# A 2x2 block of gate/up weight chunks in seven products: a macaron SwiGLU block with a mixer, 256 tokens

## The reference

```python
D_MODEL, SEQ, FFN_DIM, N_DIFF_HEADS, DEPTH = 2048, 256, 5632, 8, 1

def rms_norm(x, g):
    return x * lax.rsqrt(jnp.mean(x * x, axis=-1, keepdims=True) + 1e-6) * g

def swiglu(x, w_gate, w_up, w_down):
    return (jax.nn.silu(x @ w_gate) * (x @ w_up)) @ w_down

x = x + 0.5 * swiglu(rms_norm(x, ffn1_norm), ffn1_w_gate, ffn1_w_up, ffn1_w_down)
proj = rms_norm(x, mix_norm) @ w_in                  # 6 parts: b, c, xv, q, k, v
y_conv = short_conv_mixer(b_gate, c_gate, xv, conv_w)
y_attn = rms_norm(diff_attention(q, k, v, lam), subln_w) * (1 - lambda_init)
x = x + jnp.concatenate([y_conv, y_attn], -1) @ w_out
x = x + 0.5 * swiglu(rms_norm(x, ffn2_norm), ffn2_w_gate, ffn2_w_up, ffn2_w_down)
return rms_norm(x, final_norm)                       # (1, 256, 2048), float32
```

## Time and profile before

| | |
|---|---|
| median of 3 runs | 1829.52 us (1829.44 to 1829.53) |
| span of the profiled execution | 1827.1 us |
| around the span, to the median | 2.4 us |
| TensorE busy | 1816.5 us, 99%, 8105 matmuls |
| VectorE busy | 1015.8 us, 56% |
| ScalarE busy | 829.3 us, 45% |
| GpSimd busy | 31.3 us, 2% |
| DMA | 368 MB, mean 201 GB/s |

### The profile page before, as it was taken

One profiled execution on the slowest core, in us unless ns is written; L12 is line 12 of the kernel. 1 busy time (PEld: TensorE's weight loads), 2 busy tenths in 40 slices (PEclk: granted clock), 3 DMA queues, 4 the chain that ended last, 5 costly groups with the idle time before them and its releaser, 6 DMA issues.

```text
span 1827.1 us, 22464 instructions
## 1 busy us (share of the span) xinstructions
PE 1816.5 (99%) x8105; PEld 1500.3 (82%) x8105; DVE 1015.8 (56%) x1237; ACT 829.3 (45%) x986; POOL 31.3 (2%) x36
## 2 busy tenths in 40 slices
PE   9999999999999999999999999999999999999998
PEld 7888888888888888888888888888888888888886
DVE  6555555555545555557657766555555555554554
ACT  6444444444444444545455455444444444443443
POOL 0000000000000000000000000000000000000000
PEclk9999999999999999999999999999999999999999
DMA  7666666666666656765665566666666666655554
GB/s 258 206 207 202 203 205 206 206 203 202 206 205 207 204 195 202 224 190 179 191 207 173 192 208 209 202 205 204 206 206 199 208 203 204 209 199 195 193 195 139
DMA packets 207563, 368.03 MB, mean 201 GB/s; under 512 B 19600, under 2 KB 37648, under 8 KB 207376
## 3 DMA queue, kind: packets, MB, share of 16 engines
q1 hardware_dynamic: 206784, 365.51, 63.2%
q0 software_dynamic: 144, 1.05, 0.2%
q10 hardware_dynamic: 576, 0.69, 0.1%
HBM read 347.25 MB, written 2.10 MB: 191 GB/s over the span
## 4 chain that ended last, share of the span: by engine, by line
PE 99%; DVE 0%; ACT 0%; DMA 0%; issue 0%; DVEq 0%; ACTq 0%
PE bank L382 33%; PE bank L384 33%; PE bank L383 33%; PE bank L508 0%; PE bank L525 0%; DMA x<-in_x_dram 0%; PE bank L420 0%; PE bank L439 0%; PE bank L516 0%; PE bank L533 0%; ACT x L629 0%; DVE w_lo L814 0%; ACT w_hi L596 0%; DVE xT_lo L834 0%; DVE xT_hi L1028 0%
## 5 line engine op out<-in xcount | busy, mean ns | idle before, releaser
L814 DVE TENSOR_TENSOR w_lo<-raw,w_hi 128x1024 fp32r<-128x1024 f32 x655 | 806.4, 1232 | 774.2 <-ACT w_hi L596 773.7
L596 ACT ACTIVATE w_hi<-raw 128x1024 fp32r<-128x1024 f32 x655 | 693.7, 1060 | 910.1 <-PE bank L384 905.3
L382 PE MATMUL bank<-w_hi,xT_hi 128*128 128x512 f32 x1788 | 699.3, 391 | 1.0 <-DVE w_lo L814 1.0
L384 PE MATMUL bank<-w_hi,xT_lo 128*128 128x512 f32 x1788 | 696.1, 389 | 0.0
L383 PE MATMUL bank<-w_lo,xT_hi 128*128 128x512 f32 x1788 | 695.8, 389 | 0.0
L382 PEld LDWEIGHTS bank<-w_hi,xT_hi 128*128 128x128 f32 x1788 | 335.6, 188 | 72.4 <-issue 3.8
L384 PEld LDWEIGHTS bank<-w_hi,xT_lo 128*128 128x128 f32 x1788 | 335.6, 188 | 70.1
L383 PEld LDWEIGHTS bank<-w_lo,xT_hi 128*128 128x128 f32 x1788 | 335.7, 188 | 68.8
L382 PE MATMUL bank<-w_hi,hT_hi 128*128 128x512 f32 x704 | 273.9, 389 | 0.0
L383 PE MATMUL bank<-w_lo,hT_hi 128*128 128x512 f32 x704 | 273.9, 389 | 0.0
L384 PE MATMUL bank<-w_hi,hT_lo 128*128 128x512 f32 x704 | 273.9, 389 | 0.0
(11 more groups left out here) (115 smaller groups left out, 418.2 us busy)
## 6 DMA issues: line engine op xcount, KB each, us to landing
raw<-in_ffn_w_up_dram SPq DMA_DIRECT2D x176, 512.0 KB, 3.7
raw<-in_ffn_w_down_dram SPq DMA_DIRECT2D x176, 512.0 KB, 3.6
raw<-in_ffn_w_gate_dram SPq DMA_DIRECT2D x175, 512.0 KB, 3.5
raw<-in_w_in_dram SPq DMA_DIRECT2D x96, 512.0 KB, 4.2
raw<-in_w_out_dram SPq DMA_DIRECT2D x32, 512.0 KB, 4.1
turn_in<-gate SPq DMA_DIRECT2D x448, 32.0 KB, 2.5
x<-in_x_dram SPq DMA_DIRECT2D x3, 512.0 KB, 8.7
out_dram<-x SPq DMA_DIRECT2D x6, 256.0 KB, 2.8
```

The lines of the kernel that those rows point to most:

```text
L382: pe.matmul(acc, hi[:, kt, ts], w_hi[slot][:, kk], start=(k == 0 and kk == 0), stop=False)
L384: mm = pe.matmul(acc, lo[:, kt, ts], w_hi[slot][:, kk], start=False, stop=(k == chunks - 1 and kk == KC - 1))
L596: act.activation(w_hi[slot][:], raw[slot][:], ACT.Copy).then_inc(hi_ready, 1)
L814: dve.tensor_tensor(w_lo[slot][:], raw[slot][:], w_hi[slot][:].bitcast(F32), ALU.subtract)\
```

## The change

In groups 1 to 8 of each FFN the last two chunks of the width (KA, KB) are taken for gate and up together as a 2x2 block: rows KA, KB and columns gate, up, called b11 (gate, KA), b12 (up, KA), b21 (gate, KB), b22 (up, KB), against the 2x2 block of token tiles by KA, KB. The four block results come from seven products of 6 matmuls (P1 to P7), each on one stationary pair and one combined weight block, and not from eight. Every product has a w_hi and w_lo of its own in the rings of four, so a group has 19 forms: 12 plain ones with 12 matmuls and 7 products with 6.

VectorE builds the combined blocks in place (`outer_sums`, `first_sum`, `second_sum`, `third_sum`) and, once per FFN, the combined token tiles `s_hi`, `s_lo` (`token_sum`, `split_tokens`, in group 0). Some products belong to more than one result. Their sums so far are copied from PSUM by ScalarE (`snapshot`, four copies a group) to tiles `gate_kept` and `up_kept` while the bank goes on accumulating, and are added when the banks are drained (`gate_sum`, `up_sums`); TensorE waits for those copies at three places (`snapped`). The Silu reads the summed tile, and its product with up is one more VectorE step. The four block tiles and the kept tiles lie over the last three groups' part of `hT`, the token sums over `gfin`, whose load moves from the end of the first FFN to the start of the last stage. SP loads a group's blocks during the up phase of the group before, and moves the hidden tile in 4 DMAs behind the first up chunk and 12 behind the second. The loops over groups are unrolled on all engines; groups 0, 9 and 10 keep their form. The turning of a hidden tile moves to the end of its group, for group 0 and the mixed ones. Left out below: ring numbers in unchanged stages, the plain form (as `unit` before) and the token sums' arithmetic.

```diff
+NORM = CD - 2
+KA, KB = CD - 2, CD - 1
+P1, P2, P3, P4, P5, P6, P7 = range(1, 8)
+G0, G1, G2, AT_P1, G3, AT_P5, AT_P2, G4, AT_P6, AT_P4, G5, AT_P7, AT_P3, U0, U1, U2, U3, U4, U5 = range(19)
+AT = {P1: AT_P1, P2: AT_P2, P3: AT_P3, P4: AT_P4, P5: AT_P5, P6: AT_P6, P7: AT_P7}
+PLAIN = (G0, G1, G2, G3, G4, G5, U0, U1, U2, U3, U4, U5)
+FORMS = 2 * NORM + 7
+MIXED = range(1, GROUPS - 2)
+FFN_FORMS = FORMS * len(MIXED) + 2 * CD * (GROUPS - len(MIXED))
+def group_form(c):
+    return FORMS * len([g for g in MIXED if g < c]) + 2 * CD * len([g for g in range(c) if g not in MIXED])
...
+PRODUCT = [product_of(f) for f in range(CH_END)]
+FORM_OF_RAW = [f for f in range(CH_END) if PRODUCT[f] is None]
+RAW_OF = {f: m for m, f in enumerate(FORM_OF_RAW)}
...
+        with ExitStack() as region:
+            blocks, kept = [], []
+            for half in ("hi", "lo"):
+                part(f"hT_{half}_front", [P, KF - 3 * BT, SEQ])
+                kept.append(part(f"kept_{half}", [P, TT, W]))
+                blocks += [part(f"block_{half}{n}", [P, KC, W]) for n in range(2)]
...
+        b11, b12, b21, b22 = (b[:] for b in blocks)
+        gate_kept, up_kept = kept
+        s_f = diff[:].rearrange("p k n -> p (k n)").rearrange("p (s k n) -> p s k n", s=4, k=KC)
+        source = {P1: b11, P5: b12, P6: b11, P2: b21, P4: b21, P7: diff[:], P3: b22}
...
+            def load(f, w, pair, col):
+                m = RAW_OF[f]
+                if m >= RING:
+                    sp.wait_ge(lo_ready, FORM_OF_RAW[m - RING] + 1)
                 src = w[0].rearrange("(k p) n -> p k n", p=P)[:, KC * pair:KC * pair + KC, bass.ds(col, W)]
-                sp.dma_start(raw[slot][:], src).then_inc(raw_loaded[slot], 16)
+                sp.dma_start(raw[m % RING][:], src).then_inc(raw_loaded[m % RING], 16)
+            def load_block(ch, c, to, name, freed_by, w, pair):
+                if c > MIXED[0]:
+                    sp.wait_ge(lo_ready, ch + group_form(c - 1) + AT[freed_by] + 1)
+                src = w[0].rearrange("(k p) n -> p k n", p=P)[:, KC * pair:KC * pair + KC, c * W:(c + 1) * W]
+                sp.dma_start(to, src).then_inc(block_loaded[name], 16)
...
+            def next_blocks(base, wg, wu, c, k):
+                if c not in MIXED:
+                    return
+                if k == 1:
+                    load_block(base, c, b11, "b11", P6, wg, KA)
+                if k == 2:
+                    load_block(base, c, b12, "b12", P5, wu, KA)
+                if k == 3:
+                    load_block(base, c, b22, "b22", P3, wu, KB)
+                if k == 4:
+                    load_block(base, c, b21, "b21", P4, wg, KB)
...
+            def mixed_group(f, base, wg, wu, c):
+                b = base + group_form(c)
+                for k, at in enumerate((G0, G1, G2, G3, G4, G5)):
+                    load(b + at, wg, k, c * W)
+                for k, at in enumerate((U0, U1, U2, U3, U4, U5)):
+                    load(b + at, wu, k, c * W)
+                    if k == 0:
+                        move_hidden(f, c, 0)
+                    if k == 1:
+                        for q in range(1, QUADS):
+                            move_hidden(f, c, q)
+                    next_blocks(base, wg, wu, c + 1, k - 1)
...
+            def product(f, to, hi, lo, opens=False, seen=False, on_sums=False):
+                pe.wait_ge(lo_ready, f + 1)
+                slot = f % RING
+                acc = bank[to][:]
+                for kk in range(KC):
+                    pe.matmul(acc, hi[:, kk], w_hi[slot][:, kk], start=(opens and kk == 0), stop=False,
+                              skip_group_check=on_sums)
+                    pe.matmul(acc, hi[:, kk], w_lo[slot][:, kk], start=False, stop=False, skip_group_check=on_sums)
+                    mm = pe.matmul(acc, lo[:, kk], w_hi[slot][:, kk], start=False, stop=(seen and kk == KC - 1),
+                                   skip_group_check=on_sums)
+                mm.then_inc(chunk_used, 1)
+            def mixed_group(ch, pr, c, quad):
+                b = ch + group_form(c)
+                half = KC * KA, KC * KB
+                a11 = [x[:, half[0]:half[0] + KC, 0:P] for x in (xT_hi, xT_lo)]
+                a12 = [x[:, half[1]:half[1] + KC, 0:P] for x in (xT_hi, xT_lo)]
+                a22 = [x[:, half[1]:half[1] + KC, P:2 * P] for x in (xT_hi, xT_lo)]
+                s1, s2, s3, s4 = ((s_hi[:, n], s_lo[:, n]) for n in range(4))
+                banks_free(pr + c, 0)
+                plain(b + G0, 0, 0, opens=True)
+                plain(b + G1, 0, 1)
+                plain(b + G2, 0, 2)
+                banks_free(pr + c, 1)
+                product(b + AT[P1], 3, *a11, opens=True, seen=True)
+                plain(b + G3, 0, 3)
+                if c == MIXED[0]:
+                    pe.wait_ge(token_lo, 1 + quad // len(MIXED))
+                product(b + AT[P5], 2, *s1, opens=True, seen=True)
+                product(b + AT[P2], 0, *a12)
+                plain(b + G4, 0, 4)
+                pe.wait_ge(snapped, 4 * quad + 1)
+                product(b + AT[P6], 3, *s2, seen=True, on_sums=True)
+                product(b + AT[P4], 1, *a22)
+                plain(b + G5, 0, 5, ends=True)
+                pe.wait_ge(snapped, 4 * quad + 3)
+                product(b + AT[P7], 3, *s3, seen=True, on_sums=True)
+                product(b + AT[P3], 2, *s4, on_sums=True)
+                plain(b + U0, 1, 0, wait_for=4 * quad + 4, on_sums=True)
+                for k, at in enumerate((U1, U2, U3, U4)):
+                    plain(b + at, 1, k + 1, on_sums=True)
+                plain(b + U5, 1, 5, ends=True, on_sums=True)
...
+            def high(f):
+                if PRODUCT[f] is not None:
+                    high_product(f, *PRODUCT[f])
+                    return
+                m = RAW_OF[f]
+                act.wait_ge(raw_loaded[m % RING], ring_count(m))
+                if f >= RING:
+                    act.wait_ge(chunk_used, f - RING + 1)
+                act.activation(w_hi[f % RING][:], raw[m % RING][:], ACT.Copy).then_inc(hi_ready, 1)
...
+            def high_product(f, quad, p):
+                if p in (P1, P2, P3):
+                    act.wait_ge(block_loaded[{P1: "b11", P2: "b21", P3: "b22"}[p]], 16 * (quad + 1))
+                else:
+                    act.wait_ge(blocks_summed, 4 * quad + {P7: 1, P5: 2, P6: 3, P4: 4}[p])
+                act.wait_ge(chunk_used, f - RING + 1)
+                act.activation(w_hi[f % RING][:], source[p], ACT.Copy).then_inc(hi_ready, 1)
+            def snapshot(to, of, f, scale=1.0):
+                act.wait_ge(chunk_used, f + 1)
+                act.activation(to, bank[of][:], ACT.Copy, scale=scale).then_inc(snapped, 1)
+            def gate_summed(pair, t):
+                act.wait_ge(drained[0], pair * TT + t + 1)
+                act.activation(gate[:, t], gate_kept[:, t], ACT.Silu, scale=rstd[:, t:t + 1]).then_inc(gated, 1)
...
+            def mixed_group(ch, pr, hid, c):
+                b = ch + group_form(c)
+                high(b + G3)
+                high(b + AT[P5])
+                high(b + AT[P2])
+                high(b + G4)
+                snapshot(gate_kept[:, 0], 3, b + AT[P1])
+                high(b + AT[P6])
+                high(b + AT[P4])
+                snapshot(up_kept[:, 1], 2, b + AT[P5], scale=rstd[:, 1:2])
+                high(b + G5)
+                split_hidden(hid, c - 1)
+                high(b + AT[P7])
+                snapshot(up_kept[:, 0], 3, b + AT[P6], scale=rstd[:, 0:1])
+                high(b + AT[P3])
+                high(b + U0)
+                high(b + U1)
+                gate_summed(pr + c, 0)
+                snapshot(gate_kept[:, 1], 3, b + AT[P7])
+                high(b + U2)
+                high(b + U3)
+                gate_summed(pr + c, 1)
+                high(b + U4)
+                high(b + U5)
+                for n in range(RING):
+                    high(b + FORMS + n)
...
+            def outer_sums(quad, ch, c):
+                if c == MIXED[0]:
+                    dve.wait_ge(token_lo, 1 + quad // len(MIXED))
+                else:
+                    dve.wait_ge(lo_ready, ch + group_form(c - 1) + AT[P7] + 1)
+                dve.wait_ge(block_loaded["b12"], 16 * (quad + 1))
+                dve.wait_ge(block_loaded["b22"], 16 * (quad + 1))
+                dve.tensor_tensor(diff[:], b22, b12, ALU.subtract).then_inc(blocks_summed, 1)
+            def first_sum(quad):
+                dve.wait_ge(block_loaded["b11"], 16 * (quad + 1))
+                dve.tensor_tensor(b12, b12, b11, ALU.subtract).then_inc(blocks_summed, 1)
+            def second_sum(quad, b):
+                dve.wait_ge(lo_ready, b + AT[P1] + 1)
+                dve.wait_ge(blocks_summed, 4 * quad + 2)
+                dve.tensor_tensor(b11, b22, b12, ALU.subtract).then_inc(blocks_summed, 1)
+            def third_sum(quad, b):
+                dve.wait_ge(lo_ready, b + AT[P2] + 1)
```

(64 more changed lines are left out.)

187 lines of the change are left out of this document (134 added, 53 removed).

## The result

The changed kernel takes 1809.99 us (median; 1809.80 to 1810.29), the kernel before 1829.53 beside it: a ratio of 0.9894, 95% interval 0.9882 to 0.9907, 1.1% faster. The profiled execution has a span of 1807.5 us where before had 1827.1. The forecast was 1807.8 us within 1807.0 to 1814.0. It was 2.2 us too low, within its range; the miss is larger than the spread of the runs (0.5 us), so it has a cause.

What follows compares the result with a forecast made beforehand. TensorE's matmuls at a fixed pitch were taken as the bound; 16 x 1.360 = 21.76 us removed, all added work, queues and unrolling at 0, gives 1829.52 - 21.76 = 1807.8 us, range 1807.0 to 1814.

Steps and rivals of the forecast that it cites:

- What bounds the kernel: Whole span: TensorE, busy 99% at full clock; time is the number of matmuls times a pitch of 0.22664 us.
- What is removed: Mixed groups: 186 matmuls in place of 192, 1.360 us less a group, 21.76 us over 16 groups.
- Added work on VectorE and ScalarE: Mixed groups: extra conversions, sums and snapshots fit beside TensorE (VectorE 35.0, ScalarE 25.3 of 42.15 us); cost 0.
- the walk: One mixed group, deadline by deadline: every conversion and snapshot ready in time, 2.2 us least conversion lead at P3; no stall.
- Queues: SP's reordered loads and hidden-tile moves: last move issued at 5.6, landing 8.1, wanted 8.4 us; block loads arrive in time.
- Token sums and `gfin`: Token sums, 8.5 us in group 0's gaps of 10.4; `gfin` load at the last stage, 8 us to landing: 0.
- Unrolling: Group loops written out: returns 0.8 us at most, taken as 0.
- broken pitch: Rival: each product loses up to 0.05 us at its change of wait and bank, 5.6 us in all, 1813.4; chance 0.14.
- partial stalls: Rival: a conversion overruns its lead once a group, 8 to 16 us in all, 1816 to 1824; chance 0.08.
- nothing saved: Rival: the pitch is per form and not per matmul, so the time stays 1829.5 us; chance 0.01.
- VectorE as the bound: Rival: slower VectorE operations set the product cluster's pace; at 2.00 us each +71, 1901 us; chance 0.03.
- The branch rule: Rival: taken branches stall on instruction fetch, so unrolling gains a second time, below 1807; chance 0.01.

Runs made afterwards that it cites:

- run 8: Changed kernel with P4's six matmuls issued once more in each mixed group, into a bank nothing reads: 1831.41 us.
- run 1: Kernel before with all its group loops unrolled and nothing else changed: 1831.41 us, ratio 1.0011 to the kernel before.
- run 11: Changed kernel with VectorE's low-part subtraction done twice for eight of the nine forms in each cluster of products: 1883.92 us, ratio 1.0298 to the changed kernel.
- run 5: Kernel before with only TensorE's group loops unrolled: 1831.26 us, ratio 1.0011 to the kernel before.
- run 9: Changed kernel with TensorE's mixed groups as two passes over four and its plain groups as two passes over one: 1809.21 us.
- run 7: Changed kernel with VectorE turning a finished block right behind its drain and SP's moves one load earlier in the output projection: 1808.84 us.
- run 3: Changed kernel with 176 already satisfied wait instructions added to TensorE's first down stage: 1809.59 us.

## Why the prediction was right, and where it missed

**What bounds the kernel:** right. TensorE's matmuls at their pitch, 99% before and after.

**What is removed, 16 x 1.360 = 21.76:** right. The period is 42.16 for 42.15, the records fall by 96, each FFN shifts what follows by 10.8 us, and putting a product back costs 1.34 to 1.35 (run 8). Against the unrolled kernel before (run 1) the change is worth 1831.41 - 1809.99 = 21.4; the 0.3 that lack of 21.76 are as much as the wait at the last reciprocal, below.

**Added work on VectorE and ScalarE at 0, the walk:** right to 0.2 us at each of three deadlines, and run 11 shows that the leads are real and how large they are. The sums of durations (35.0 and 25.3) were 1.6 and 1.2 too high, since operations back to back start closer than they last; on the safe side, as said there.

**Queues:** right in effect. The hidden moves come 0.46 us too late for ScalarE where the walk had them 0.3 early; nothing behind ScalarE noticed. The walk had SP done with the moves 1.9 us too early (5.6 for 7.5); that they came only 0.6 late is owed to the last one landing 1.3 us behind SP's last issue, where the walk took 2.5. Token sums and `gfin`: nothing to be seen of either on the path.

**Unrolling, "returns 0.8 us at most, and I take 0":** this term was mis-sized, and its bound had the wrong sign. It costs 1.9 to 2.2 us (runs 5 and 1), all of it TensorE's as far as the runs can tell. The trace of before had no stall in a loop pass, so the prediction was right that no branch had to be won back; it did not ask what the longer program does to stages that don't change. It looked at the loops, and the loss lies in the output projection (1.2) and behind the last store (0.5). The price was bounded only on the side of a gain, 0.8 us; a bound for a loss was missing. The term that it needed is the least lead of the unchanged stages, 1.35 us at the handover to the second FFN. That the measured time still lies in the range is room left for other things (broken pitch, small stalls): no rival had unrolling as a loss. The rule of the Trainium skill weighed there (Runtime: NRT & Kernel Launch, Instruction fetch mechanics), that kernels prefer full unrolling, is wrong for this kernel by the measured 2 us: with loops again (49 packets in place of 63) it is 0.8 us faster, 0.6 when each is set against the kernel before beside it. The same section gives instruction fetches in blocks of 16 KiB; with 1.03 MB in 63 packets the trace agrees.

**The rest, 0.37 us** at the last reciprocal, is in every kernel with the mixed groups and in none without, unrolled or not. What VectorE waits for there ended 0.46 us before (ScalarE's root, 0.30 us long from 1800.29). Its cause was not tried and stays open. Open too is how unrolled loops of TensorE make loads land up to 0.8 us later in a stage whose program and number of packets are the same: run 9 halved the added packets and the loads of the down stages still took 4.5 us to land, as in the changed kernel.

**Rivals:** broken pitch, partial stalls and nothing saved are excluded by the period; VectorE as the bound needs the eight extra operations of run 11. The branch rule would have made the unrolled kernel faster; it is slower (runs 1 and 5).

## What to carry to other kernels

Price a change of the program's form (unrolling, a longer body) by the stages it doesn't touch: look there for the handover with the least in hand, since a later landing shows where it exceeds the lead (here 2.3 us late with 1.35 in hand). A cure at that handover (run 7) and a shorter program (run 9) gave back 1.9 of 2.2 us, and the first is the better one, because it covers any delay up to its 1.9 us, whatever the cause. When products are made cheaper than their conversions, walk the cluster deadline by deadline; the engine's share of the span (66% here, 71% when it was already the bound) says nothing about it.

## What the runs showed of the hardware

- Writing TensorE's loops out added 27 instruction packets of 16 KB (37 to 64), 0.01% of all packets, and the median landing of a 512 KB load in an unchanged stage went from 3.9 to 4.7 us, with 8 instruction packets in that stage in both. SP's loops written out added none to this queue.
- A loop body of four groups on TensorE (744 matmuls with their weight loads, and waits) was fetched once for two passes.
- Waits that are already met cost TensorE nothing: 176 wait instructions more, no slower (run 3).
- A batch of four 32 KB moves holds SP for 2.41 us, and for 2.75 to 3.50 when one of TensorE's instruction packets is fetched meanwhile: 19 of 156 batches in thirteen traces, each with a packet, and none of the others.
